# A 1-core two-block transformer kernel: the first attention's woven units dealt in finer parts, and both convolution feed-forward blocks in narrow up units alone

## What is computed

```python
def conv_ffn(xn, up_w, conv_w, conv_b, down_w):        # both layers of the first block
    h = causal_dwconv(xn @ up_w, conv_w, conv_b)       # 3 taps over time, per channel
    g, u = h[..., :D_FF], h[..., D_FF:]                # D_FF = 2816
    return (jax.nn.silu(g) * u) @ down_w

def diff_attention(...):                               # layer 1; 8 heads, 2 blocks of 128 queries
    ...
        p = jax.nn.softmax(sc, axis=-1)
        attn = p[:, :, 0] - lam * p[:, :, 1]
        outs.append(jnp.einsum("bhqk,bkhe->bqhe", attn.astype(v.dtype), vc))
    o = rmsnorm(o, subln_g) * (1.0 - lambda_init)
    return o.reshape(b, s, H * ATTN_V_DIM).astype(xn.dtype) @ out_w

mkv = mem_n @ mem_w_kv[l]                              # second block: keys and values of a memory
```

## Time and profile before

| | |
|---|---|
| median of 3 runs | 1889.17 us (1886.53 to 1890.65) |
| the profiled execution | 1889.49 us, its span 1887.8 us, so 1.7 us lie around the span |
| mean granted TensorE clock | 0.985 of full |
| PE busy | 1826.0 us, 97% |
| DVE busy | 1346.9 us, 71% |
| ACT busy | 1004.4 us, 53% |
| DMA | 310 MB, mean 164 GB/s |

### The profile page before, as it was taken

One profiled execution on the slowest core, in us unless ns is written; L12 is line 12 of the kernel. 1 busy time (PEld: TensorE's weight loads), 2 busy tenths in 40 slices (PEclk: granted clock), 3 DMA queues, 4 the chain that ended last, 5 costly groups with the idle time before them and its releaser, 6 DMA issues.

```text
span 1887.8 us, 32266 instructions
## 1 busy us (share of the span) xinstructions
PE 1826.0 (97%) x12953; PEld 1703.2 (90%) x12953; DVE 1346.9 (71%) x1704; ACT 1004.4 (53%) x1204; POOL 5.3 (0%) x34
## 2 busy tenths in 40 slices
PE   6989999999999999999999999999999999999998
PEld 6988899999889899989999999998988998999997
DVE  5968668888788678886667666666756666776665
ACT  5744455566656555665445445444545445665443
POOL 1000000000000000000000000000000000000000
PEclk9999999999999899999999999999999999999999
DMA  6632155555534355556555554555646554446552
GB/s 190 190 123 90 46 178 178 180 198 187 174 114 134 113 178 176 180 179 200 190 177 174 169 183 137 198 178 185 195 134 199 180 197 139 156 135 201 186 177 82
DMA packets 237954, 310.39 MB, mean 164 GB/s; under 512 B 8226, under 2 KB 213800, under 8 KB 237864
## 3 DMA queue, kind: packets, MB, share of 16 engines
q1 hardware_dynamic: 236520, 308.03, 49.4%
q10 hardware_dynamic: 1344, 1.09, 0.2%
HBM read 308.04 MB, written 1.06 MB: 164 GB/s over the span
## 4 chain that ended last, share of the span: by engine, by line
PE 75%; DVE 11%; issue 8%; ACT 4%; DVEq 1%; DMA 0%; ACTq 0%; SPq 0%
PE ps L628 17%; PE ps L630 9%; PE ps L656 8%; PE ps L658 7%; PE ps L659 7%; PE ps L607 7%; PE ps L609 7%; PE ps L608 7%; DVE weights_lo L1801 3%; DVE scratch L1951 2%; ACT scratch L1310 2%; ACT weights_hi L1185 2%; DVE scratch L1854 1%; DVE scratch L1847 1%; PE ps L890 1%
## 5 line engine op out<-in xcount | busy, mean ns | idle before, releaser
L1801 DVE TENSOR_TENSOR weights_lo<-raw_weights,weights_hi 128x2048 fp32r<-128x2048 f32 x283 | 647.7, 2289 | 246.5 <-ACT weights_hi L1185 245.3
L628 PE MATMUL ps<-normed,weights_hi 128*128 128x512 f32 x1984 | 705.2, 399 | 3.9 <-DVE normed L1894 2.4
L1185 ACT ACTIVATE weights_hi<-raw_weights 128x2048 fp32r<-128x2048 f32 x283 | 539.0, 1906 | 235.0 <-DVE scratch L1854 97.7
L630 PE MATMUL ps<-normed,weights_lo 128*128 128x256 f32 x1984 | 557.7, 281 | 0.0
L628 PEld LDWEIGHTS ps<-normed,weights_hi 128*128 128x128 f32 x1984 | 373.6, 188 | 94.9 <-DVE weights_lo L1801 2.7
L656 PE MATMUL ps<-down_in_hi,weights_hi 128*128 128x256 f32 x1440 | 412.9, 287 | 10.8 <-DVE down_in_lo L1915 7.0
L658 PE MATMUL ps<-down_in_lo,weights_hi 128*128 128x256 f32 x1440 | 409.9, 285 | 0.0
L659 PE MATMUL ps<-down_in_hi,weights_lo 128*128 128x256 f32 x1440 | 409.8, 285 | 0.0
L630 PEld LDWEIGHTS ps<-normed,weights_lo 128*128 128x128 f32 x1984 | 375.7, 189 | 0.1
L607 PE MATMUL ps<-normed,weights_hi 128*128 128x256 f32 x1216 | 358.7, 295 | 9.9 <-DVE normed L1894 7.2
L609 PE MATMUL ps<-normed,weights_lo 128*128 128x256 f32 x1216 | 346.3, 285 | 0.0
(11 more groups left out here) (251 smaller groups left out, 1342.1 us busy)
## 6 DMA issues: line engine op xcount, KB each, us to landing
raw_weights<-in_ffn_w_gate_up_dram SPq DMA_DIRECT2D x88, 1024.0 KB, 5.0
raw_weights<-in_ffn_up_w_dram SPq DMA_DIRECT2D x44, 1024.0 KB, 5.0
raw_weights<-in_ffn_w_down_dram SPq DMA_DIRECT2D x44, 1024.0 KB, 4.9
raw_weights<-in_ffn_down_w_dram SPq DMA_DIRECT2D x22, 1024.0 KB, 4.9
raw_weights<-in_ssd_in_w_dram SPq DMA_DIRECT2D x20, 1024.0 KB, 5.3
raw_weights<-in_a_w_in_dram SPq DMA_DIRECT2D x14, 1024.0 KB, 5.0
raw_weights<-in_attn_in_w_dram SPq DMA_DIRECT2D x12, 1024.0 KB, 5.1
raw_weights<-in_ssd_out_w_dram SPq DMA_DIRECT2D x8, 1024.0 KB, 4.9
```

The source lines that it names most:

```text
L628: mm(ps[:, b + a, :], wh[:, k, a * P:(a + 1) * P], h[:, k, :, :].rearrange("p c t -> p (c t)"), start=(k == 0), stop=False, skip_group_che ...
L630: last = mm(ps[:, b + a, 0:T], wl[:, k, a * P:(a + 1) * P], h_hi[:, k, :], start=False, stop=(k == DK - 1), skip_group_check=True)
L1185: f(w_hi[:, s, :], raw[:, s, :], ACT.Copy).then_inc(hi_split.sem, hi_split.plus())
L1801: tt(w_lo[:, s, :], raw[:, s, :], f32(w_hi[:, s, :]), ALU.subtract).then_inc(lo_split.sem, lo_split.plus())
```

## The change

The first attention's seven woven units are dealt in eighths (one of the eight input blocks each), four and three by turns over all 16 steps (`KV_PARTS`). ACT and DVE follow a table of the steps in which a unit ends (`KV_ENDS`): one step after it ACT splits and DVE evacuates, two and three steps after it DVE splits in two halves. The inputs of the first two output down units are fed within steps 13 and 15 (`KV_FED`), and half of the first output down unit (the middle four of its eight blocks) is put between the last turn and the last values. `o_sum(3)` moves behind the second down unit. Both convolution feed-forward blocks get a PE program of their own, `conv_ffn`, with all 11 pairs narrow, in banks 4, 5 and 6, 7 by turns; a unit waits until the one that used its bank four units earlier is taken out. ACT and DVE do no `copy_low`, `merge` and `scale` there.

```diff
-KV_WOVEN = 7
+KV_PARTS = (4, 3) * 8
+KV_ENDS = {-1: 0, 2: 1, 4: 2, 6: 3, 8: 4, 11: 5, 13: 6, 15: 7}
+KV_FED = {13: 0, 15: 1}
...
+            def conv_ffn():
+                def pair(b):
+                    for a in range(2):
+                        pe.wait_ge(evacuated.sem, evacuated.value(-3))
+                        up_unit(b=b + a, reused=False)
...
+                down_unit(first=True)
+                with c.repeat((FU - 3) // 2 - 1, {lo_split: 6, evacuated: 4, su_done: 6, hid_ready: 2}):
+                    for b in (4, 6):
+                        pair(b)
+                        down_unit()
+                pair(4)
+                down_unit()
+                pair(6)
+                pair(4)
+                for j in range(3):
+                    down_unit(last=(j == 2))
...
             def diff_step(t):
-                kv_units(t)
+                part = sum(KV_PARTS[:t])
+                for k in range(part, part + KV_PARTS[t]):
+                    up_unit(ks=range(k % DK, k % DK + 1), b=4 + k // DK % 2)
...
-            softmax_attention(("diff",), diff_step)
-            down_unit(first=True)
-            o_sum(3)
+            def first_out():
+                down_unit(first=True, ms=range(2, 6), end=False)
+            softmax_attention(("diff",), diff_step, first_out)
+            down_unit(first=True, ms=(0, 1, 6, 7), begin=False)
             pe.wait_ge(evacuated.sem, evacuated.value())
             turn_memory(4, 0, 0)
             turn_memory(5, 0, 1)
             down_unit()
+            o_sum(3)
             down_unit()
             pe.wait_ge(bank_free.sem, bank_free.next(2))
...
             def diff_step(t):
-                kv_units(t)
+                if t - 1 in KV_ENDS:
+                    dve.wait_ge(su_done.sem, su_done.next())
+                    to_memory(KV_ENDS[t - 1], None)
                 if t in (9, 13, 17):
                     norm_heads((t - 9) // 4)
+                for part in (0, 1):
+                    if t - 2 - part in KV_ENDS:
+                        split_part(part)
+                if t in KV_FED:
+                    feed(heads_out, KV_FED[t], (out_slot + KV_FED[t]) % RING)
```

More of the change, by code:

```diff
@@ L702, in downs, with ffn @@
                 down_unit(last=True)
[L704 to L708, removed]
+            def ffn(stats=True):
+                wide_unit(4, first=True)
+                if stats:
+                    wide_unit(6, ks=range(DK // 2))
                     norm_sum(b=FFN_STAT)
[L710 to L726 removed]
+                    wide_unit(6, ks=range(DK // 2, DK))
+                else:
+                    turn_small(FOX_HEADS, FFN_STAT)
+                    wide_unit(6)
+                wide_unit(0)
+                wide_unit(6, reused=True)
+                pe.wait_ge(evacuated.sem, evacuated.value(-1))
                 down_unit(first=True)
@@ L1357, in ffn @@
                 gate(0, renewed=ahead)
-                up(0, conv is None)
+                up(0)
                 give((first + 1) % RING)
-                trip(1, (first + 1) % RING, 0, conv is None)
+                trip(1, (first + 1) % RING, 0)
                 u0 = unit[0]
@@ L1585, in _ @@
             copy_values(TURNED_BEFORE_DIFF, False)
-            kv_units = woven(KV_WOVEN, ahead=True)
+            heads_out, out_slot = proj[:, 24:32, :], (slot[0] + 8) % RING
             def o_square(i):
@@ L2004, in trip @@
                     split_next()
-                gate(0, renewed=ahead, wide=conv is None)
-                up(0, 6 if conv is None else 5, conv is None)
+                even, odd = ((4, 6), (4, 6)) if wide else ((4, 5), (6, 7))
+                gate(0, renewed=ahead)
+                up(0, even[1])
                 give((first + 1) % RING)
-                trip(1, (first + 1) % RING, (0, 6) if conv is None else (6, 7), conv is None)
-                u0 = unit[0]
-                with c.repeat(FU - 5, per_trip(**extra)) as i:
-                    trip(i + 2, (first + 1) % RING)
-                unit[0] = u0 + 3 * (FU - 5)
-                trip(FU - 3, first)
-                for j in (FU - 2, FU - 1):
-                    gate(j)
-                    up(j)
+                trip(1, (first + 1) % RING, (0, 6) if wide else odd)
+                u0, twice = unit[0], (FU - 5) // 2
+                with c.repeat(twice, {t: 2 * n for t, n in per_trip(**extra).items()}) as i:
+                    trip(i * 2 + 2, (first + 1) % RING, even)
+                    trip(i * 2 + 3, (first + 1) % RING, odd)
+                unit[0] = u0 + 6 * twice
+                trip(FU - 3, first, even)
+                for j, banks in ((FU - 2, odd), (FU - 1, even)):
+                    gate(j, banks[0])
+                    up(j, banks[1])
                     give((first + j - FU) % RING)
@@ L2371, in to_memory @@
                    rows(rstd[:], 2), ALU.mult).then_inc(evacuated.sem, evacuated.plus())
-            kv_units = woven(KV_WOVEN, to_memory, 1, ahead=True)
+            heads_out, out_slot = proj[:, 24:32, :], (slot[0] + 8) % RING
             turned.n += 4
```

69 lines of the change are left out of this document (44 added, 25 removed).

## The result

The changed kernel takes **1875.72 us** (median of 5 runs, 1875.43 to 1881.36) against 1887.56 for the kernel before (5 runs, 1886.47 to 1890.65): ratio 0.9942, 95% interval 0.993 to 0.9954. Of the 6.1 us between the forecast of 1881.8 and the median, 1.6 are the kernel before itself: the forecast started from a median of 1889.17, and these five runs have 1887.56. The profiled execution of the changed kernel happened to be the longest of the five, 1881.36; a second trace, taken later, is one of 1877.18. Both are used.

A forecast was written before the change was run, and what follows sets the result against it. PE was taken as the bound, busy in nearly all the span. Attention -5.3 and convolution blocks -2.1 gave -7.4, so 1882.1, stated as 1881.8 us for the median; range 1878.5 to 1887.5 for 8 in 10.

The forecast's parts named there:

- Narrow units, +3.8: Convolution blocks on PE: 36 units made narrow cost 0.105 us more each, +3.8 us, nearly all on the path.
- the fourth rival: Narrow units cost less than the rows say: 1878.0 with none of the 3.8 paid, 1879.4 at 1.4; chance 0.07.
- Block ends, -5.9: Last three down units of both convolution blocks: fewer DVE merges remove losses of 3.67 and 2.19 us.
- Steps, +0.3: PE waits within the attention steps, taken at step 14: +0.3 us, from a range of 0 to 2.
- Attention's end, -9.77: From last woven half to end of first down unit: 9.77 us lost to waits and lower clock, all going.
- the memory wait, +2.7: Second set of transposes waits for DVE's memory-value copies because the last sum over heads moves later: +2.7 us.
- The clock behind the memory wait, +1.5: Lower PE clock after the wait at the second set of transposes: +1.5 us, bounds 0 and 1.7.
- 1889.5 - 7.4: Whole kernel: profiled execution less attention's -5.3 and convolution's -2.1, giving 1882.1 us for a like execution.
- its clock terms: Lower-clock parts of the forecast: 1.5 added behind the memory wait; 1.48 and 1.46 removed at first block's and attention's ends.
- The waits didn't move: Rival: attention waits only move as DVE and ACT bound the steps, 1889.3 us; chance 0.08.
- the ends weren't late: Rival: convolution block ends stay late because ACT's tap sets DVE's pace, 1887.7 us; chance 0.09.
- no step wait: Rival: PE waits in steps 5, 7, 9, 13, about 1.5 + 1.5 us each, up to 1893.8; chance 0.08.

The follow-up runs named there:

- attention part alone: Kernel before with only the first attention's part of the change, both convolution blocks as before: 1883.97 us, ratio 0.9973.
- the delay of 1.7 us: Changed kernel with four repeated sums, result unused, on PE between the first convolution block and the attention: 1882.28 us, ratio 0.9962.
- the feeds late: Changed kernel with feeds and first output down unit back behind the 16 steps, woven units still in eighths: 1889.78 us, ratio 1.0007.
- the delay of 3.0: Changed kernel with seven repeated sums on PE between the first convolution block and the attention: 1883.07 us, ratio 0.9974.
- four and seven sums: Four or seven repeated sums on PE ahead of the attention; in the kernel before 1890.07 and 1890.88 us, in the changed kernel 1882.28 and 1883.07.
- convolution part alone: Kernel before with only the convolution feed-forward blocks in narrow units, attention as before: 1887.28 us, ratio 0.999.
- narrow-ends version: Changed kernel, last sum mid-down-unit, convolution loop wide, only first two and last two pairs narrow: 1871.82 us; with four added sums 1875.86.

## Why the prediction was wrong

Its steps, one after the other:

- *Narrow units, +3.8.* Held. A unit takes 5.76. From the first down unit of the layer before to the last three of the first block it is 438.09 - 217.94 = 220.15 us, and in the trace of the attention part alone, where the loop is wide, 218.38: +1.8 a block, so +3.5. The shorter gap for 256 columns that the Trainium skill ("TensorE: Matmul & The Clock Gate", Back-to-back issue gap) gives for a matmul by itself, the basis of the fourth rival, is not what this kernel shows: 0.120 us again in the loop's matmuls, each with its own weight load.
- *Block ends, -5.9.* Held to the last digit: 17.28 and 17.28.
- *Steps, +0.3.* About nothing: between 551 and 633 us PE's timeline shows no wait at all.
- *Attention's end, -9.77, and the memory wait, +2.7.* Held: the wait is 2.62. From block 1's end to block 2's last down units the first traces have 819.31 - 455.54 = 363.77 before and 358.46 after, -5.3 with 1.8 of narrow units against it, so -7.1; forecast without the clock term -6.8. Not held is the size of the loss in the kernel before: its first down unit behind the 3.57 took 7.22 us in the trace that the prediction read and 8.48, 8.31 and 7.98 in its three others. The 1.46 lost there was the cheapest case of four.
- *The clock behind the memory wait, +1.5.* **This is the first step that failed.** I took it from the falls behind 2.40 and 3.57 in one trace, with 1.79 as the only case without, as though the length of a wait decided. The same wait of 2.62 has a fall in the attention part alone, with the delay of 1.7 us and, 1.4 us later, with the feeds late, and none in both traces of the changed kernel nor with the delay of 3.0. So 0 was measured where 1.5 was charged. The bound of 0 was in the working, and the range of the forecast itself went down to 1880.0 for it.
- *"1889.5 - 7.4": that everything outside the changed stages stays as it was.* **This is the second, and about as large.** It stood in no term. Nearly all waits outside did stay, at the same sizes, but not the clock behind them.

How large is each? First by stages. The changed ones run from the first down unit of the layer before the first convolution block to the end of the second block, 831.11 - 217.94 = 613.17 us in the first trace of the changed kernel. The starts of these in the first trace of the kernel before (its end is in the earlier trace rows) and of the changed kernel:

```profile
216.22 0.36 PE L656 MATMUL ps<-down_in_hi,weights_hi 128*128 128x256 f32 x1
```

```profile
217.94 0.36 PE L658 MATMUL ps<-down_in_hi,weights_hi 128*128 128x256 f32 x1
```

Start and end in the second traces, of the kernel before and of the changed one:

```profile
219.07 0.36 PE L656 MATMUL ps<-down_in_hi,weights_hi 128*128 128x256 f32 x1
...
843.15 0.40 PE L628 MATMUL ps<-normed,weights_hi 128*128 128x512 f32 x1
```

```profile
217.56 0.36 PE L658 MATMUL ps<-down_in_hi,weights_hi 128*128 128x256 f32 x1
...
830.73 0.40 PE L630 MATMUL ps<-normed,weights_hi 128*128 128x512 f32 x1
```

All in us; the sums of a delay, which stand in the changed stages, are taken off:

| traces | changed stages | rest of the span |
|---|---|---|
| kernel before | 622.56, 624.08 | 1265.2, 1265.4 |
| the same with four and seven sums | 622.9, 622.6 | 1263.7, 1262.3 |
| changed kernel | 613.17, 613.17 | 1266.5, 1262.3 |
| the same with four and seven sums | 614.7, 613.2 | 1265.4, 1265.1 |
| attention part alone | 618.5 | 1262.5 |
| convolution part alone | 620.5 | 1265.1 |

The 614.7 holds the fall behind the memory wait. Without a delay the changed stages gave 9.4 to 10.9 us instead of 7.4: 1.5 because the clock term was not paid, 0.5 from the small sizes above, and up to 1.5 from the larger falls in the kernel before. The rest of the span is 1.3 us longer in the changed kernel's first trace and 3.1 shorter in its second; the changed kernel has both the longest and nearly the shortest, with the same instructions. Only the means of the runs say that it tends to the short end. As an estimate, with these stages: 1889.05 - 1.7 - 623.0 = 1264.3 before and 1877.2 - 1.7 - 613.2 = 1262.3 after, so 2 us of the missing 4.5 lie outside.

Then by clock. In each trace I added up, behind every wait, what the matmuls that start 0.21 apart lost against 0.12. The kernel before lost 11.4 and 12.2 us in its two traces, the changed one 9.4 and 5.5, the attention part alone 10.2, the convolution part alone 10.6. With that taken off the executions' times, 1878.1 and 1879.0 are left of before, 1872.6 of the attention part, 1876.7 of the convolution part, 1872.0 and 1871.6 of the changed kernel: -6.0 and -1.9 for the parts and -6.8 for the whole. The parts add up to within 1.1, about as well as the count can tell, for it leaves out slow rows of other forms (the transposes behind the memory wait took 1.98 us in the attention part alone and 0.85 in the changed kernel). The forecast without its clock terms (1.5 to come, 1.48 and 1.46 to go) was -6.0.

The share of the clock that wasn't granted, times the span, points the same way over all runs: on average 23.6 us before, 21.1 with the attention part, 23.1 with the convolution part, and 16.5 in the changed kernel; 19.1 and 19.4 in the changed kernel with the delays; 16.4 in the narrow-ends version, and 19.1 with the delay. It is a hint and no size. In the kernel before with four sums it is 21.1, against 23.9 on the same chip without them, though the time rose. And it does not cover the start of the kernel alike. The same matmuls start 0.21 apart from 17 us on in the first traces of the changed kernel and of the kernel before, but the windows show a full clock in one and the half in the other:

```profile
16.96:20.70 3.74, 3.74 (x17) 3.74 (x18) 3.74 (x9) 2.91 (x7) 0.00 (x0) 1.00 0.60 147
```

```profile
16.92:20.70 3.78, 3.77 (x18) 3.78 (x19) 3.78 (x9) 2.94 (x7) 0.00 (x0) 0.50 0.57 136
```

So the structure gave about what was forecast for it, 6 to 7 us where the terms without clock said 6.0, and the clock gave some 5 where the terms said 1.4. The changed kernel's waits happen to lie so in time that fewer of them are followed by the lower clock. That unrelated delays of 1.7 and 3.0 us cost it some 3 us beyond themselves, and give the kernel before about 1 back, shows that much of this hangs on timing and not on either part. **What stays open** is what about the spacing decides: a fall follows the same wait or doesn't at places that differ by a microsecond, and in two executions of the same kernel. The length of the wait alone doesn't explain it, nor does the clock in the wait itself: in its two halves it was 1.00 and 0.98 in the attention part alone, where the fall came, and 1.00 and 1.00 in the changed kernel, where none did. The Trainium skill ("TensorE: Matmul & The Clock Gate", What's actually happening) has the activity judged in windows that run free of the kernel, so that where in such a window a stretch of work lands decides, and differs from run to run. What the delays and the pairs of traces show fits that rule; the windows themselves no run here shows.

Of the rivals none came true. The waits didn't move, the ends weren't late, there was no step wait and no cheaper narrow unit. What was missing from the list is a gain or loss in clock at waits that the change leaves as they are.

## What to carry to other kernels

Work out an edit's structure from the starts of rows and expect it to hold to a few tenths, but give a separate term, of either sign and several falls wide, to the clock behind every wait of the whole kernel, since anything that shifts those waits in time may change it. Before believing (or discarding) a gain of a few microseconds, time both kernels again with the same small delay in each, and read the delay's length from the trace (four sums meant as 1.0 us took 1.7): here that turned 11.8 into 8.4 and 7.3, and showed that the narrow-ends version's further 5.4 is real. Spreading cover work finer paid only together with inputs that were fed early, and trading PE time for DVE time pays only in the units where DVE is late.

## What the runs showed of the hardware

- Behind waits of 1.79 to 3.57 us the matmuls go on at 2.4 GHz or at 1.2; a fall costs 1.2 to 2.7 us, mostly about 1.5. Behind the wait of 1.79 at the first block's end the clock fell in all four traces of the kernel before, with and without a delay, behind that of the same length at the second block's end in none of them, but with the attention part alone behind both (1.5 us lost each).
- Two executions of one kernel differ by up to 6 us with the same instructions; between the two traces of the changed kernel, 4.2 us apart, nearly all of it arises behind the waits of 3.39 and 2.41, each with a fall in one trace and none in the other. One more pair, behind a wait of 2.78 at 112 us: the first trace of the changed kernel, then its second.

```profile
112.07:116.10 4.03, 4.03 (x22) 4.03 (x23) 2.02 (x5) 2.86 (x3) 0.00 (x0) 0.62 0.03 5
```

```profile
113.44:117.40 3.96, 3.96 (x33) 3.96 (x34) 1.95 (x5) 2.79 (x3) 0.00 (x0) 1.00 0.02 4
```

- A sum of 256 columns in plain float32 takes PE 0.43 us (four take 1.73), where a product of the weight units of the same width takes 0.12.
- 1.7 us of added PE work cost 4.5 us in one kernel, 4.4 in another and 1.0 in a third.
